# PEER value stage in one pass over the experts, with weights made once and partial sums emptied by VectorE

## The reference, cut to what matters

```python
h2 = rmsnorm(x, norm2_g[l]) * (1.0 + scale2) + shift2
x = x + gate2 * peer(h2, ...)
# peer, for each block of tokens: 8 heads x 16 chosen experts per token
a = jnp.einsum("td,thkd->thk", xb, u[eb])
act = gb * jax.nn.gelu(a)
return jnp.einsum("thk,thkd->td", act, v[eb])
```

## Time and profile before

| | |
|---|---|
| median of 3 runs | 3388.33 us (3387.2 to 3395.19) |
| profiled execution: its time, its span | 3392.54 us, 3390.7 us |
| PE, busy share of the span | 94% |
| DVE (VectorE) | 77% |
| ACT (ScalarE) | 33% |
| POOL (GpSimd) | 22% |
| DMA, mean over the span | 261 GB/s |
| V stage, first to last matmul | 2298.9 to 3386.6 us of the span |

### The profile page before, as it was taken

How to read it: one execution, slowest core, us unless ns; L and a number is a source line. 1 busy time by engine, 2 the same in 40 slices (tenths; PEclk the granted TensorE clock), 3 DMA queues, 4 the chain that set the end, 5 groups by cost and what they waited for, 6 DMA issues and landing times.

```text
span 3390.7 us, 45823 instructions
## 1 busy us (share of the span) xinstructions
PE 3182.5 (94%) x17301; PEld 2923.6 (86%) x17301; DVE 2618.8 (77%) x3067; ACT 1109.7 (33%) x1032; POOL 754.0 (22%) x444
## 2 busy tenths in 40 slices
PE   4898967879899999999999999999999998999999
PEld 3686744457678999999999999999999998999999
DVE  6996968856763688888778888866777776777777
ACT  3323233431122444444323333332333332333332
POOL 4500000000020012222102322313333332333333
PEclk8899989979999999999999999999999999999999
DMA  8621213247744357777648888888999998999997
GB/s 348 252 92 69 81 56 130 111 162 299 269 161 165 134 197 278 277 277 277 228 169 327 340 343 334 344 305 318 349 343 348 347 347 324 349 347 348 348 347 283
DMA packets 241097, 883.66 MB, mean 261 GB/s; under 512 B 17680, under 2 KB 132496, under 8 KB 169744
## 3 DMA queue, kind: packets, MB, share of 16 engines
q1 hardware_dynamic: 161552, 545.82, 43.1%
q0 software_dynamic: 55296, 268.46, 21.2%
q10 hardware_dynamic: 24192, 68.64, 5.3%
HBM read 824.13 MB, written 58.72 MB: 260 GB/s over the span
## 4 chain that ended last, share of the span: by engine, by line
PE 78%; DVE 14%; DMA 3%; ACT 2%; issue 2%; POOL 0%; DVEq 0%; SPq 0%; ACTq 0%; PEldq 0%
PE bank L1362 12%; PE bank L1363 12%; PE bank L1364 12%; PE bank L1687 10%; PE bank L1688 10%; PE bank L1689 10%; PE bank L1662 2%; DVE w_lo L783 2%; DVE ada_w L808 2%; PE bank L1573 2%; PE bank L1574 2%; PE bank L1575 2%; DVE qk_rstd L976 1%; DMA ada_w<-wada 1%; DVE ada_w L792 1%
## 5 line engine op out<-in xcount | busy, mean ns | idle before, releaser
L783 DVE TENSOR_TENSOR w_lo<-w_raw,w_hi 128x2048 fp32r<-128x2048 f32 (+1 forms) x319 | 727.2, 2280 | 590.8 <-ACT w_hi L427 579.0
L427 ACT ACTIVATE w_hi<-w_raw 128x2048 fp32r<-128x2048 f32 (+1 forms) x327 | 621.6, 1901 | 1336.5 <-PE bank L1364 626.4
L1362 PE MATMUL bank<-act_hi,w_hi 128*128 128x384 f32 (+1 forms) x2584 | 908.0, 351 | 45.8 <-DVE w_lo L783 27.8
L1363 PE MATMUL bank<-act_lo,w_hi 128*128 128x384 f32 (+1 forms) x2584 | 900.0, 348 | 0.0
L1364 PE MATMUL bank<-act_hi,w_lo 128*128 128x384 f32 (+1 forms) x2584 | 899.9, 348 | 0.0
L1687 PE MATMUL bank<-wt_hi,w_hi 128*128 128x384 f32 x2048 | 687.9, 336 | 17.5 <-DVEq L1323 8.4
L1688 PE MATMUL bank<-wt_lo,w_hi 128*128 128x384 f32 x2048 | 685.8, 335 | 0.0
L1689 PE MATMUL bank<-wt_hi,w_lo 128*128 128x384 f32 x2048 | 685.8, 335 | 0.0
L417 POOL DMA_INDIRECT v_row<-v,vrow_i x256 | 401.3, 1568 | 734.9 <-DVE y_g L1308 655.1
L1362 PEld LDWEIGHTS bank<-act_hi,w_hi 128*128 128x128 f32 x2584 | 490.2, 190 | 78.2 <-issue 24.9
L1364 PEld LDWEIGHTS bank<-act_hi,w_lo 128*128 128x128 f32 x2584 | 489.7, 190 | 22.2
(11 more groups left out here) (244 smaller groups left out, 3128.6 us busy)
## 6 DMA issues: line engine op xcount, KB each, us to landing
w_raw<-u SPq DMA_DIRECT2D x128, 1024.0 KB, 8.1
w_raw<-v SPq DMA_DIRECT2D x128, 1024.0 KB, 5.3
ada_w<-wada SPq DMA_DIRECT2D x80, 1024.0 KB, 5.1
gelu_l<-gelu_scratch SPq DMA_DIRECT2D x64, 768.0 KB, 6.5
gate_l<-gate_scratch SPq DMA_DIRECT2D x64, 768.0 KB, 9.5
w_raw<-win SPq DMA_DIRECT2D x27, 1024.0 KB, 4.7
gelu_scratch<-gelu_s ACTq DMA_DIRECT2D x128, 192.0 KB, 5.6
gate_scratch<-g_chunk ACTq DMA_DIRECT2D x8, 3072.0 KB, 13.4
```

The lines of the kernel that those rows point to most:

```text
L427: act.activation(w_hi[n0 % 2][:, 0:width], w_raw[n0 % 2][:, 0:width], ACT.Copy).then_inc(hi_done, 1)
L783: dve.tensor_tensor(w_lo[s][:, 0:width], w_raw[s][:, 0:width], w_hi[s][:, 0:width].bitcast(F32), ALU.subtract).then_inc(lo_done, 1)
L1362: pe.matmul(out, wh, hi_t(k), start=(k == 0), stop=False)
L1363: pe.matmul(out, wh, lo_t(k), start=False, stop=False)
```

## The change

The V stage runs once over the experts. `v_index` gives the order of the 128 tiles of v: for each group of 2 units (8 blocks of experts), 4 jobs for one half of the channels and then 4 for the other, with the order turned at each group, so that the halves follow each other as A, BB, AA, BB and so on. Where the half changes, after 8 jobs (the first time after 4), the 8 banks are emptied: TensorE waits for its own last sums (`seg_sum`), and VectorE adds each bank times gate2 straight into `acc_o`, which was loaded with the whole residual (`add`, 128x384, 15 times 8 of them). The last close of each half is as before (`close_half`, 128x512).

The weights of a unit are made once, 32 units in all, into 4 buffers each for `wt_hi` and `wt_lo`, but through one `wt` and one `gate_l`; the gelu is loaded into `wt` and multiplied in place, and the next unit's load waits for `weigh_lo` of the one before. `v_step` adds whole rows (128x2048), 128 of them, gathered from a new input `v_rows` with the row numbers of u's gather into the 3 buffers `u_row`; the row numbers for the half rows fall away. The gathers no longer wait for the end of the U stage, the first units' weights are made during its last jobs, and the second unit's load and its `hi` and `lo` steps are ordered between the first loads of v. The loops of all engines hold 16 jobs instead of 4, and run 7 times.

```diff
+def v_index(q):
+    group, pos, j = q // 8, q // 4 % 2, q % 4
+    return 64 * (pos ^ (group % 2)) + 4 * group + j
...
-        wt_hi = [at(f"wt_hi{s}", 112 + 6 * s, [P, 4, TD], F32R) for s in range(2)]
-        wt_lo = [at(f"wt_lo{s}", 124 + 6 * s, [P, 4, TD], F32R) for s in range(2)]
...
-        gelu_l = [at(f"gelu_l{s}", 148 + 6 * s, [P, 4, TD]) for s in range(2)]
-        gate_l2 = [at(f"gate_l2{s}", 176 + 6 * s, [P, TD // GC, 4, GC]) for s in range(2)]
-        v_row = [at(f"v_row{s}", 4 * s, [P, 1024]) for s in range(4)]
...
-        out_s = at("out_s", 32, [P, 8, T])
...
+        wt_hi = [at(f"wt_hi{s}", 112 + 6 * s, [P, 4, TD], F32R) for s in range(4)]
+        wt_lo = [at(f"wt_lo{s}", 136 + 6 * s, [P, 4, TD], F32R) for s in range(4)]
+        wt = at("wt", 176, [P, 4, TD])
+        gate_l = at("gate_l", 182, [P, TD // GC, 4, GC])
+        acc_o = at("acc_o", 0, [P, KD, T])
+        y_g = at("y_g", 204, [P, D])
...
+            def load_unit(n, turn=0):
+                if n:
+                    sp.wait_ge(wtl_ready, n + turn * 4)
+                rows = bass.ds(turn * 16 + 4 * n, 4)
+                sp.dma_start(wt[:], gelu_d[rows].rearrange("e p t -> p e t")).then_inc(wt_loaded, 16)
+                sp.dma_start(gate_l[:], gate_d[:, :, rows, :].rearrange("c p i t -> p c i t")).then_inc(wt_loaded, 16)
+            def load_v(q, turn=0):
+                load_w(J_V + q, v_d[v_index(q) + turn * 8], turn=turn * 8)
             for s in range(2):
                 sp.wait_ge(g_stored[s], DMA_LEAD + 16 * 4)
                 sp.wait_ge(gelu_stored[s], DMA_LEAD + 16 * 4)
                 sp.wait_ge(hot_used[2 * s + 1], LEAD + 24)
...
+            load_unit(0)
+            load_v(0)
+            load_unit(1)
+            load_v(1)
             for s in range(2):
                 sp.wait_ge(gelu_stored[s], DMA_LEAD + 16 * NKEY // 2)
...
+            load_v(2)
+            load_v(3)
+            load_unit(2)
+            for q in range(4, 8):
+                load_v(q)
+            load_unit(3)
+            with sp.Fori(0, 7) as i:
+                for r in range(16):
+                    load_v(8 + r, i)
+                    if r % 4 == 2:
+                        load_unit(4 + r // 4, i)
+            for q in range(120, 128):
+                load_v(q)
...
             pool.wait_ge(rows_ready, 1)
             for n in range(P):
...
                     pool.wait_ge(dots_done, n - 2)
                 pool.indirect_dma_start(u_row[n % 3][:], None, urow_d, bass.IndirectOffsetOnAxis(ap=urow_i[:, n:n + 1], axis=0)).then_inc(
                     u_row_loaded[n % 3], 16)
-            pool.wait_ge(pe_jobs, J_V)
             pool.wait_ge(dots_done, P)
-            for n in range(2 * P):
-                if n >= 4:
-                    pool.wait_ge(y_g_steps, n - 2)
-                pool.indirect_dma_start(v_row[n % 4][:], None, rows_of_v, bass.IndirectOffsetOnAxis(ap=vrow_i[:, n % P:n % P + 1], axis=0),
-                                        element_offset=(n // P) * (NKEY * P) * 1024).then_inc(v_row_loaded[n % 4], 16)
+            for n in range(P):
+                if n >= 3:
+                    pool.wait_ge(y_g_steps, n - 1)
+                pool.indirect_dma_start(u_row[n % 3][:], None, vrow_d, bass.IndirectOffsetOnAxis(ap=urow_i[:, n:n + 1], axis=0)).then_inc(
+                    v_row_loaded[n % 3], 16)
...
+            def weigh_hi(n, turn=0):
+                act.wait_ge(wt_ready, n + 1 + turn * 4)
+                act.activation(wt_hi[n % 4][:], wt[:], ACT.Copy).then_inc(wth_ready, 1)
...
+            weigh_hi(0)
+            gelu_pair(63)
+            weigh_hi(1)
+            act.dma_start(acc_o[:], x1_d).then_inc(x1_loaded, 16)
+            for q in range(2, 6):
+                hi(J_V + q)
+                if q == 4:
+                    weigh_hi(2)
+            with act.Fori(0, 7) as i:
+                for r in range(16):
+                    hi(J_V + 6 + r, i * 8)
+                    if r % 4 == 0:
+                        weigh_hi(3 + r // 4, i)
+            for e in range(10):
+                hi(J_V + 118 + e)
+                if e == 0:
+                    weigh_hi(31)
+                if e == 7:
+                    for d in range(0, 8, 2):
+                        act.wait_ge(y_ready, d + 2)
+                        act.dma_start(out_d[:, 8 + d:10 + d, :], acc_o[:, 8 + d:10 + d, :]).then_inc(out_stored, 16)
+            for d in range(0, 8, 2):
+                act.wait_ge(y_ready, 8 + d + 2)
+                act.dma_start(out_d[:, d:d + 2, :], acc_o[:, d:d + 2, :]).then_inc(out_stored, 16)
...
-            T_.step(dve.tensor_copy(e1_u[:], e1_g[:]))
-            T_.step(dve.tensor_scalar(e1_u[:], e1_u[:], 1, None, ALU.bitwise_and))
             T_.step(dve.scalar_tensor_tensor(out=row_f[:], in0=e1_g[:], scalar=float(P), in1=e2_g[:], op0=ALU.mult, op1=ALU.add))
-            T_.mark(dve.tensor_copy(urow_i[:], row_f[:]))
-            T_.step(dve.tensor_tensor(row_f[:], row_f[:], e2_g[:], ALU.add))
-            T_.step(dve.tensor_copy(vrow_f[:], e1_u[:]))
-            T_.step(dve.scalar_tensor_tensor(out=vrow_i[:], in0=vrow_f[:], scalar=-127.0, in1=row_f[:], op0=ALU.mult, op1=ALU.add))
+            T_.step(dve.tensor_copy(urow_i[:], row_f[:]))
...
+            def weigh(n, turn=0):
+                dve.wait_ge(wt_loaded, (n + 1) * 32 + turn * 128)
+                w = wt[:].rearrange("p i (c t) -> p i c t", c=TD // GC)
+                dve.tensor_tensor(w, w, gate_l[:].rearrange("p c i t -> p i c t"), ALU.mult).then_inc(wt_ready, 1)
+            def weigh_lo(n, turn=0):
+                dve.wait_ge(wth_ready, n + 1 + turn * 4)
+                dve.tensor_tensor(wt_lo[n % 4][:], wt[:], wt_hi[n % 4][:].bitcast(F32), ALU.subtract).then_inc(wtl_ready, 1)
+            dve.wait_ge(hot_ready[1], 24)
+            dve.memset(y_g[:], 0.0).then_inc(y_g_steps, 1)
             for n in range(122, NKEY):
                 lo(J_U + n)
                 if n in (123, 124):
                     dot(n + 3)
+                if n == 126:
+                    weigh(0)
+            weigh_lo(0)
+            lo(J_V)
+            weigh(1)
+            lo(J_V + 1)
+            weigh_lo(1)
             dve.wait_ge(act_g_ready, 1)
             T_.step(dve.tensor_tensor(gate_g[:], gate_g[:], a_g[:], ALU.mult))
...
+            def v_step(m, turn=0):
+                dve.wait_ge(v_row_loaded[m % 3], 16 * (m // 3 + 1) + turn * 96)
+                dve.wait_ge(y_g_steps, m + 1 + turn * 18)
+                dve.scalar_tensor_tensor(out=y_g[:], in0=u_row[m % 3][:], scalar=gate_g[:, bass.ds(turn * 18 + m, 1)], in1=y_g[:],
                                          op0=ALU.mult, op1=ALU.add).then_inc(y_g_steps, 1)
...
+            def add(k, half_i, turn=0):
+                if k > 1:
+                    dve.wait_ge(added, 8 * (k - 1) + turn * 16)
                 for d in range(8):
...
+                    dve.wait_ge(seg_sum, 8 * k + d + 1 + turn * 16)
+                    m = 8 * half_i + d
+                    o = acc_o[:, m, 0:TD]
+                    dve.scalar_tensor_tensor(out=o, in0=bank[d][:, 0:TD], scalar=mod[:, 5 * KD + m:5 * KD + m + 1], in1=o,
+                                             op0=ALU.mult, op1=ALU.add).then_inc(added, 1)
+            def close_half(half_i, order, k):
+                dve.wait_ge(added, 8 * k)
+                for d in range(8):
+                    dve.wait_ge(y_sum, 8 * order + d + 1)
+                    m = 8 * half_i + d
+                    dve.scalar_tensor_tensor(out=acc_o[:, m, :], in0=bank[d][:], scalar=mod[:, 5 * KD + m:5 * KD + m + 1], in1=acc_o[:, m, :],
                                              op0=ALU.mult, op1=ALU.add).then_inc(y_ready, 1)
...
+            for q in range(2, 6):
+                if q == 5:
+                    dve.wait_ge(x1_loaded, 16)
+                    add(0, 0)
+                lo(J_V + q)
+                if q == 2:
+                    v_step(0)
+                if q == 3:
+                    v_step(1)
+                if q == 4:
+                    weigh(2)
+                if q == 5:
+                    weigh_lo(2)
+            with dve.Fori(0, 7) as i:
+                for r in range(16):
+                    if r % 8 == 7:
+                        add(1 + r // 8, 1 - r // 8, i)
+                    lo(J_V + 6 + r, i * 8)
+                    if r % 4 == 0:
+                        weigh(3 + r // 4, i)
+                    v_step(2 + r + (r > 3) + (r > 11), i)
+                    if r % 4 == 1:
+                        weigh_lo(3 + r // 4, i)
+                    if r in (3, 11):
+                        v_step(3 + r + (r > 3), i)
+            dve.wait_ge(y_g_steps, P + 1)
+            dve.sem_inc(y_g_ready, 1)
+            for e in range(10):
+                if e == 7:
+                    close_half(1, 0, 14)
+                lo(J_V + 118 + e)
+                if e == 0:
+                    weigh(31)
+                if e == 1:
```

(89 more changed lines are left out.)

101 lines of the change are left out of this document (3 added, 98 removed).

## The result

The change made the kernel slower. Its median is 3464.9 us (3461.86 to 3466.25, 4 runs) against 3391.76 us for the kernel before on the same chip (3387.2 to 3397.01, 4 runs): a ratio of 1.0206, 95% interval 1.0184 to 1.0227. The forecast was 3377 us, its range 3368 to 3402. The profiled execution took 3466.25 us, with a span of 3464.5 us.

What follows compares the result with a forecast made beforehand. TensorE, busy 94% of the span, was taken as the bound. From the profiled 3392.5 us, -15.9 + 9.2 - 3.0 - 2.0 = -11.7 gave 3380.8; with medians 4.2 us lower, about 3377 us, range 3368 to 3402.

Steps and rivals of the forecast that it cites:

- A rival: TensorE's longer V loop doesn't stay in instruction memory and is fetched again: 12 to 41 us, about 3401 us; chance 0.27.
- TensorE, just drained, waits for a fetch at 6 back edges: 2.0 us ... to 5.3 us: Price of each jump back in the V loop if its first piece of code was overwritten, before 1.5 us of slow clock.
- those of nearly two stay whole: Argument against refetching the V loop's code: existing loops nearly two pieces long are not fetched again.
- my two readings: V loop's code: by 128 KiB of memory it fits barely, 3377 us; by a window of 2 pages it doesn't, about 3401.
- One pass, -15.9: Middle of the V stage: the change of pass, 17.4 us, goes, less small costs at the closes; bounds 12.3 to 17.4.
- Drains, +9.2: Changes of half in the V stage: 15 more waits of 0.55 us plus 1 us at the branch; bounds 4.5 to 15.
- dearer drains: Rival: each wait of TensorE for its own result costs 1.0 us, giving 3383 us, no change; chance 0.12.
- VectorE's adds hidden: Changes of half: 8 adds take about 4.3 us and TensorE doesn't wait, with some 1.5 us of cover.
- Weights once, whole rows, nothing: V stage: halved loads and weight work win nothing, as TensorE wasn't waiting for either; DMA at 315 GB/s.
- Row numbers, -3.0: Near 1240 us: fewer small VectorE operations shorten TensorE's wait from 3.62 to 2.2 us, with fewer slow matmuls; bounds 1.4 to 4.1.
- Start, -2.0: Start of the V stage: third tile of v some 2 us earlier, second gap mostly closes; bounds 4.1 less to 2.3 more.

Runs made afterwards that it cites:

- moved kernel: Changed kernel with the last turn of TensorE's U loop written out, so the V loop touches 7 pieces of code instead of 8: 3388.97 us, ratio 0.9988.
- moved one without drains: Changed kernel with the V loop moved to touch 7 pieces, and TensorE no longer waiting for its own last results: 3375.46 us, ratio 0.9945.
- written-out run: Changed kernel with TensorE's seven turns of 16 V jobs written out, without loop or branch, drains kept: 3388.44 us, ratio 0.9988.
- late load: Moved kernel without drains, with ScalarE's 4 MB residual load issued after its copy of the third V tile: 3379.5 us, ratio 0.9949.
- 16-job run: Kernel before with TensorE's V loop of 16 jobs a turn instead of 4, no drain at the branch: 3412.8 us, ratio 1.0056.

## Why the prediction was wrong

*Where it failed: the loop's code.* The sum of the forecast has no term for it. A rival had the mechanism and the place, 6 back edges; I gave it 0.27 and priced it at 12 to 41 us. It costs 74 us, 12.4 us an edge: between the changed and the moved kernel six turns differ by 6 x (147.37 - 135.01) = 74.2 us, and the other 3 of the 77.3 us (1165.6 - 1088.3) lie at the start of the stage, where the second gap is 4.0 us in the one and 1.0 in the other. The step that failed in size is "TensorE, just drained, waits for a fetch at 6 back edges: 2.0 us ... to 5.3 us". That price was read from transfers of 256 KB and 1 MB; the piece of 16 KB takes 1.1 us, and the branch still stands for 6.3 us. Two more things were left out: a fetch after a drain starts late, so the first gap is 7 to 8 us and not 3.3; and the loop begins a few instructions ahead of a boundary of pieces, so a second fetch of 2.5 to 4 us stands behind the first, with the clock at 1.2 GHz between and after them. The step that failed in judgement is "those of nearly two stay whole", taken for evidence on a loop of over six; loops of 4.7 pieces stay too, so neither of my two readings gave the limit. For loops of this length it is the number of pieces touched, 7 or 8.

The Trainium skill (Runtime: NRT & Kernel Launch, section Instruction fetch mechanics) gives TensorE's memory as 128 KiB, 8 pieces of 16 KB. By that figure 1590 instructions fit; the runs show that a loop touching 8 pieces does not stay. Its rule of a window of 2 pages is not what loops of 12 and of 16 jobs show here: they touch 6 and 7 pieces and jump back without a gap.

Why 7 and not 8 is not shown. One reading fits: in every turn of the changed kernel q8 carries 9 pieces, one more than the loop touches, and one of them begins 5 to 7 us ahead of the branch. If that is the piece behind the loop's end, fetched ahead, it takes a place that the loop's first piece would need. No run tests this.

*The other steps.* With the code out of the way, the sum can be held against the moved kernels. I cut the V stage at the last product of its fourth job, so that the start stands apart: that product begins 37.3 us behind the stage's first in the kernel before, 39.1 in the changed kernel, 36.0 in the moved and 36.3 in the moved one without drains.

- One pass, -15.9: the drainless moved kernel's V stage is 17.5 us shorter than before, 1.0 of it at the start, so 16.5. The change of pass took 17.4 us, and the close of the stage is 0.9 us longer. Right. (Its 8.4 us were a wait of the last job's second half, ahead of the first product there, L1687, and not of the transposes alone.)
- Drains, +9.2: 14.3 in the V stage, 13.5 in the medians, near the upper bound of 15. From one matmul to the next it is 0.82 us in the middle of a turn and 1.19 at a back edge, so 0.65 and 1.02 above the pitch instead of 0.55. In the written-out run, where the counts are constants, it is 0.64, so 0.47. The rival "dearer drains" had nearly this.
- VectorE's adds hidden: right. 8 take 4.29 us, and without drains no product waits for one in the loop.
- Weights once, whole rows, nothing: right; 311 GB/s against the 315 forecast, and 1.9 us of idle time before `y_g`.
- Row numbers, -3.0: right as far as the trace tells, -2.6 in the run that has them alone; the gap in the changed kernel is 2.29 us, 2.2 forecast. The two profiles reach the V stage at the same time all the same, so it is lost in the scatter of the earlier stages.
- Start, -2.0: wrong in its sign, +1.8 in the changed kernel. The second gap is 3.97 us with 11 matmuls at the slow pitch behind it, because the third tile of v is late; ScalarE's row says that it waits for this DMA, beside which 4 MB of residual are loaded. I had put it 2 us earlier although I named that load. That the residual is the cause is shown only in the moved kernels, where the late load takes the second gap away.

Together, for the V stage: -16.5 + 14.3 + 1.8 + 74.2 = +73.8, and measured 1165.6 - 1091.8 = +73.8. The parts are read from the same profiles, so that they add up is no test by itself; the code and the drains are tested by the runs that take each away. (The bounds of the forecast's terms add up to -21 and +4, not -27 and +6; nothing hangs on it.)

Had the code cost nothing, the change would have gained 4 us and not 11.7: the moved kernel, which is the change as intended, measures 0.9988. One edit more, no drains, makes it 0.9945.

## What to carry to other kernels

Before a loop of an engine is made longer, count its instructions and where it begins and ends in the compiled program: here 7 pieces of 256 ran for free and 8 cost 12.4 us a turn, and 194 instructions written out ahead of the loop were worth 76 us in the medians. Read the "issue" waits together with the code queue's row; gaps with no releaser that recur once a turn are the sign, and the price is not that of the transfer. Let the last result of a job signal for itself instead of draining an engine to be able to count.

## What the runs showed that I had not expected

- The same loop of 16 jobs, twice in one program, was fetched again in one place and not in the other, by 0.3 of a piece in its position (25.96 against 38.23).
- Code run straight through costs nothing visible: the V stage written out has no gap behind its start but for its drains, with DMA at 314 GB/s beside it (2650 to 2770 us).
- At a back edge whose code is gone, the first two pieces come one after the other, each with a gap: 7.0 and 4.0 us drained, 3.3 and 3.6 us undrained, 3.3 and 1.3 us in the 16-job run. The last difference stays open.
